# The fifth product's weights loaded ahead of the fourth product's, in the second gate of a hybrid decoder on one Trainium2 core

## The reference, cut

```python
proj = rmsnorm(x, ln_g) @ w_in
q, k, v, z_a, x_b, z_b, g_a, g_b = jnp.split(proj, SPLIT_IDX, axis=-1)
o_a = group_norm(retention(q, k, v), gn_g) * silu(z_a)
o_b = rglru(causal_conv(x_b)) * silu(z_b)
merged = sigmoid(g_a) * (o_a @ w_a) + sigmoid(g_b) * (o_b @ w_b)
return x + merged @ w_o, S_new, conv_new, h_last
```

## Time and profile before

| what | us |
|---|---|
| median of 3 runs | 1902.77 |
| profiled execution, whole | 1901.83 |
| its span, first to last instruction | 1900.0 |
| TensorE busy | 1880.8 |
| VectorE busy | 1262.8 |
| ScalarE busy | 807.3 |
| GpSimd busy | 284.6 |

### The profile page before, as it was taken

One profiled execution on the slowest core, in us unless ns is written; L12 is line 12 of the kernel. 1 busy time (PEld: TensorE's weight loads), 2 busy tenths in 40 slices (PEclk: granted clock), 3 DMA queues, 4 the chain that ended last, 5 costly groups with the idle time before them and its releaser, 6 DMA issues.

```text
span 1900.0 us, 32236 instructions
## 1 busy us (share of the span) xinstructions
PE 1880.8 (99%) x12984; PEld 1762.9 (93%) x12984; DVE 1262.8 (66%) x2144; ACT 807.3 (42%) x1293; POOL 284.6 (15%) x399
## 2 busy tenths in 40 slices
PE   8999999999999999999999999999999999999998
PEld 7899898898899999999998988988989999999997
DVE  8775665665766877864487656657557678878445
ACT  5432332423427776542344324234124377766223
POOL 2221120120231200100022201202102422001000
PEclk9999999999999999999999999999999999999999
DMA  6435544453443333543354445534544533327332
GB/s 219 129 125 166 160 149 128 164 178 110 149 150 93 107 104 97 154 124 120 99 174 158 147 124 172 178 110 149 169 126 137 165 102 111 95 83 193 103 123 78
DMA packets 114786, 257.48 MB, mean 136 GB/s; under 512 B 11822, under 2 KB 52254, under 8 KB 114510
## 3 DMA queue, kind: packets, MB, share of 16 engines
q1 hardware_dynamic: 84350, 156.00, 26.4%
q0 software_dynamic: 30144, 99.41, 16.5%
q10 hardware_dynamic: 144, 0.00, 0.0%
HBM read 196.55 MB, written 49.12 MB: 129 GB/s over the span
## 4 chain that ended last, share of the span: by engine, by line
PE 87%; DVE 5%; ACT 3%; DMA 2%; DVEq 1%; issue 1%; ACTq 1%; SPq 0%
PE bank L1944 20%; PE bank L1946 20%; PE bank L1945 20%; PE bank L2014 4%; PE bank L2015 4%; PE bank L2016 4%; PE last L2032 2%; DMA w_raw<-in_w_units 1%; PE last L2014 1%; PE last L2015 1%; PE last L2016 1%; PE bank L2282 1%; PE bank L2285 1%; PE bank L2284 1%; PE sums L2147 1%
## 5 line engine op out<-in xcount | busy, mean ns | idle before, releaser
L1944 PE MATMUL bank<-xn_hi,w_hi 128*128 128x296 f32 (+1 forms) x2176 | 650.8, 299 | 0.4 <-DVE w_lo L531 0.3
L1946 PE MATMUL bank<-xn_lo,w_hi 128*128 128x296 f32 (+1 forms) x2176 | 646.4, 297 | 0.0
L1945 PE MATMUL bank<-xn_hi,w_lo 128*128 128x296 f32 (+1 forms) x2176 | 645.7, 297 | 0.0
L1944 PEld LDWEIGHTS bank<-xn_hi,w_hi 128*128 128x128 f32 x2176 | 409.2, 188 | 7.0 <-issue 4.3
L1945 PEld LDWEIGHTS bank<-xn_hi,w_lo 128*128 128x128 f32 x2176 | 409.6, 188 | 1.0
L1946 PEld LDWEIGHTS bank<-xn_lo,w_hi 128*128 128x128 f32 x2176 | 408.8, 188 | 0.0
L524 ACT ACTIVATE w_hi<-w_raw 128x1024 fp32r<-128x1024 f32 x229 | 241.0, 1056 | 347.0 <-DMA w_raw<-in_w_units 344.5
L531 DVE TENSOR_TENSOR w_lo<-w_raw,w_hi 128x1024 fp32r<-128x1024 f32 x229 | 280.7, 1229 | 88.9 <-ACT w_hi L524 82.1
L1944 PE MATMUL bank<-oa_hi,w_hi 128*128 128x296 f32 (+1 forms) x512 | 153.7, 300 | 0.0
L1945 PE MATMUL bank<-oa_hi,w_lo 128*128 128x296 f32 (+1 forms) x512 | 151.9, 297 | 0.0
L1946 PE MATMUL bank<-oa_lo,w_hi 128*128 128x296 f32 (+1 forms) x512 | 151.7, 296 | 0.0
(11 more groups left out here) (331 smaller groups left out, 3543.6 us busy)
## 6 DMA issues: line engine op xcount, KB each, us to landing
w_raw<-in_w_units SPq DMA_DIRECT2D x199, 512.0 KB, 3.6
S<-in_state_ret POOLq DMA_DIRECT2D x64, 512.0 KB, 4.8
out_ret_s<-S POOLq DMA_DIRECT2D x64, 512.0 KB, 6.2
w_raw<-in_w_units SPq DMA_DIRECT2D x122, 256.0 KB, 3.2
vst<-v_scr SPq DMA_DIRECT2D x8, 512.0 KB, 4.1
out_ret_p<-Sp POOLq DMA_DIRECT2D x8, 512.0 KB, 5.7
w_raw<-in_w_units POOLq DMA_DIRECT2D x16, 256.0 KB, 4.7
v_scr<-vtok_hi SPq DMA_DIRECT2D x16, 160.0 KB
```

The source lines that it names most:

```text
L1944: pe.matmul(ps, w_hi[:, slot, cols], x_hi, start=first, stop=False)
L1945: pe.matmul(ps, w_lo[:, slot, cols], x_hi, start=False, stop=False)
L1946: return pe.matmul(ps, w_hi[:, slot, cols], x_lo, start=False, stop=last)
```

## The change

The parts take another order of places within a pair: A11, S1, S2, S3, A12, S4, A22. The part of the weights for the fifth product (S3) takes the fourth place, that for the fourth product (A12) the fifth. The order in which TensorE, VectorE, ScalarE and GpSimd work is as it was. The half slot of a part, the count of its landing semaphore and the part for whose end a load waits follow the new order of places: the load at a place waits for the part that held the place eight before.

```diff
+LOAD_ORDER = (A11, S1, S2, S3, A12, S4, A22)
...
+def part_place(n):
+
+    return n // PRODUCTS * PRODUCTS + LOAD_ORDER.index(n % PRODUCTS)
+
+
 def part_slot(l, n):
 
-    return (n + RING * l) % PART_RING
+    return (part_place(n) + RING * l) % PART_RING
...
         def part_arrived(l, n):
 
-            return 16 * sum(1 for m in range(l + 1) for k in range(PART_UNITS if m < l else n + 1)
-                            if part_slot(m, k) == part_slot(l, n))
+            return 16 * sum(1 for m in range(l + 1) for k in range(PART_UNITS)
+                            if (m < l or part_place(k) <= part_place(n)) and part_slot(m, k) == part_slot(l, n))
...
             def load_parts(l):
 
-                for n in range(PART_UNITS):
-                    if n < PART_RING:
-                        sp.wait_ge(unit_done, l * UNITS_LAYER + B_AT - RING + n // 2 + 1)
+                taken_by = [n // PRODUCTS * PRODUCTS + LOAD_ORDER[n % PRODUCTS] for n in range(PART_UNITS)]
+                for place, n in enumerate(taken_by):
+                    if place < PART_RING:
+                        sp.wait_ge(unit_done, l * UNITS_LAYER + B_AT - RING + place // 2 + 1)
                     else:
-                        sp.wait_ge(part_done, l * PART_UNITS + n - PART_RING + 1)
+                        sp.wait_ge(part_done, l * PART_UNITS + taken_by[place - PART_RING] + 1)
```

## The result

The changed kernel took 1909.01 us, median of 6 runs (1908.22 to 1909.69), beside 1902.48 for the kernel before (6 runs, 1902.13 to 1903.42): a ratio of 1.0034, 95% interval 1.0024 to 1.0044. It is slower by 6.5 us; the forecast was 2.4. The profiled execution has a span of 1906.8 us, 6.8 more.

The account below looks back on a forecast made before the run. TensorE bounds the kernel, busy 1880.8 of 1900.0 us. Costs of S4's later landing, 0.8 + 0.4 + 0.44 (less the 0.36 gain) + 0.8 = 2.4 us, on 1902.77 gave 1905.2 us; range 1901.7 to 1907.0.

Parts of the forecast that it names:

- The path: VectorE waits for S4's landing; behind it stand S4's sum, low halves of S2 and A12, ob_lo, S3's low half, then TensorE.
- x: Delay of S4's landing, its load now issued behind A12's at S3's end: taken as +0.8 us, between -0.36 and +1.6.
- The upper bound of 1.6: Most that S4's landing could be delayed: longest landing, 5.0 us, plus 0.48 of issue, less 3.87.
- The 0.36 of gain: Layer 1, pair 1: S3's earlier load removes VectorE's wait for S3's high half, the whole sure gain, 0.36 us.
- Pair by pair: Costs with S4 0.8 us later: pairs 1 and 2, 0.8 and 0.4 in layer 0, 0.44 and 0.8 in layer 1; pair 3, nothing.
- x is paid in full: Layer 0, pair 1: VectorE is busy from S4's sum until S3's low half, no stall to spare, so cost 0.8 us.
- Slower beyond the measurement: S3's adding load starts about 2 us sooner, beside S1's and the loads released at S3's end: 6.4 us, 1909.2; 13 in 100.
- its sign: In the profile after, S1's or S2's low half becomes what TensorE waits for if the adding loads collide; no size given.

Follow-up runs that it names:

- the second time: The changed kernel run and profiled again, on one chip beside three other kernels: 1908.93 us, +5.9 against the kernel before, ratio 1.0031.
- the kernels without the overlap: The changed kernel with S3's load held (1903.27 us), its adding load held (1902.66, or 1905.04 to A22's end), or S3's second load left out (1902.17).
- the copying transfer: The changed kernel with S3's second load on GpSimd copying in place of adding: 1905.37 us, +2.2 against the kernel before, ratio 1.0009.
- the swap in two pairs of four: The kernel before with S3's load ahead of A12's in pairs 1 and 3 only, S4's released alone: 1903.98 us, +1.2, ratio 1.0009.
- one wait: The changed kernel with S3's adding load held on GpSimd to the end of S4 of the pair before: 1902.66 us, -0.4, ratio 0.9999.

## Why the prediction was wrong

It forecast slower by 2.4 us within a range up to 1907.0, and gave 0.85 to no measurable change. It was slower by 6.5.

- **The path held, up to its end.** VectorE's wait for S4 grew, the sum for S4, the low halves and ob_lo behind it moved, and TensorE stalled for w_lo. But it stalled for S2's first, where the forecast had S3's alone. The block's growth of 6.3 us is seen in the products themselves.
- **The failing term is x.** I took +0.8 from "the queues are about as full after as before and the service time is the nearest row". The share of queues over 40 us is indeed what it was (q1 49.9%, q0 25.4%, to the earlier trace rows), and it was the wrong row: a mean over 40 us says nothing of loads that now coincide. Measured x is 1.62 and 2.88 in pair 1, and 2.16 and 2.55 the second time. The upper bound of 1.6, built from the longest landing of the trace before, was no bound either: landings of 6.2 us appeared. Of two loads released together the second is also issued 0.38 us behind the first (790.13 and 790.51 after) and not 0.48, as its own issue takes 0.43; that moves the bound to 1.5 and changes nothing else.
- **What x was made of.** A12's place ahead of S4, which I priced at 0.83 from the service time, costs 0.0 to 1.2 in pair 1 of the kernels without the overlap. That price was fair. The missing part is S3's adding load. In the sum I counted its lead as a gain of 0.36 and nothing else; it should have had a price of its own, as an issue that is moved past S4's on another queue.
- **The 0.36 of gain** in layer 1, pair 1 was real as a wait (VectorE no longer waits for S3's high half there) and worth nothing, as VectorE was late anyway.
- **Pair by pair.** Priced were 0.8 and 0.4 for pairs 1 and 2 of layer 0, 0.44 and 0.8 in layer 1, nothing for pairs 3. The profile has 1.6 and 0.1, 3.1 and 0.7, and 0.7 and 0.0 for pairs 3. For layer 0, pair 1 the rule "x is paid in full" was right: x was 1.62 and the stalls of S2, A12 and S3 grew by 0.79, 0.06 and 0.75. For pair 3 I looked at S3's slack alone. S4's sum reads the raw half of S2, and S2's low half overwrites it, so a late S4 also holds S2, whose turn comes two products sooner: S2 of pair 3 stalled by 0.67 us in layer 0. The same goes for the 2.10 of S2 in layer 1, pair 1.
- **The rival.** "Slower beyond the measurement" named this mechanism, priced it at 6.4 us (1909.2, measured 1909.01) and got 13 in 100. That its figure came out to 0.2 us is luck: it had 1.6 for each of the pairs that measured 1.6 and 0.7, 1.2 for those with 0.1 and 3.1, and 0.4 for each pair 3. The mechanism was not luck, and its sign, S2's low half as what TensorE waits for, came as written. I held against it that "bytes and mean share stay, and landings of 5 us were the rare ones". Both were true and neither spoke to it: the plain landings of 4.88 and 4.55 us in the earlier trace rows were those of loads in flight beside S1's adding load, and the change puts the issue of S3's adding load within 0.8 us of every release of S4's load.
- **Not settled.** How much of S4's delay comes from S1's adding load and how much from S3's; why the copying transfer leaves S4 as late as the adding one in layer 0 and less so in layer 1; and why the swap in two pairs of four costs 1.2 us in time where its profile's blocks grew by 2.4 (91.8 against 89.4); its interval reaches to 3.4.

## What to carry to other kernels

A load that is moved earlier takes its followers with it: here a plain load's lead of 1.6 us started an adding load on another engine's queue some 3 us sooner, on top of the one before it and of the next urgent load. Look at which transfers will be in flight at the same time, and hold the non-urgent one by a wait: one wait gave back all of 5.9 us. A share of the queues over tens of us can't price such a coincidence. The landing times of those loads that already overlap, given to every load that now will, are a nearer price, but no bound: the longest before was 5.0 us, and 6.2 came.

## What the runs showed of the hardware

Beside two adding loads of 256 KB, 2.3 us apart, and a plain load released with it, a plain load of 256 KB took 6.24 us to land (1726.74 to 1733.00 in the chain of the changed kernel), where 5.0 was the longest and 3.3 the median before. A plain load released 1.6 us later, and so further behind an adding load, was seen only 0.44 later. A second transfer that copies cost less (+2.2 us) than one that adds (+6.5 and +5.9). After TensorE had idled for 1.94 us its granted clock was at the lower level for 3.4 us; after idling for 1.62 us, in the second profile, it stayed at the upper one. The Trainium skill (DMA: Bandwidth & Descriptors, section "Queues, rings and completion order") has each DMA engine serve its rings in turn, a packet of one and then a packet of another. The traces agree so far: plain loads of the sync engine (queue q1) land later beside adding loads of GpSimd (queue q0), though they stand in different queues: S4 took 5.59 us with one adding load issued at its release, and 3.95 before. That packets alternate no run here shows.
